# A hybrid encoder step on one core: the sample's attention moved behind the third block's heads

## What is computed

```python
h = x @ w_in                                  # columns q | k | v | u, 512 each
# group A: stick-breaking attention, 8 heads x 64, strictly causal
z = (q @ k.T) * HD ** -0.5
log_1m = where(mask, log_sigmoid(z) - z, 0)
after = reverse_cumsum(log_1m) - log_1m
a_out = where(mask, exp(log_sigmoid(z) + after), 0) @ v
# group B: trailing means of u over 2, 4, 8, 16 frames, minus the token, times pool_w, scaled
mix = concat([a_out, p_out]) @ w_out
x1 = layer_norm(ALPHA * x + mix, ln1_g, ln1_b)
y = layer_norm(ALPHA * x1 + (silu(x1 @ w_gate) * (x1 @ w_up)) @ w_down, ln2_g, ln2_b)
```

## Time and profile before

| what | value |
|---|---|
| median of three runs | 2768.33 us |
| the profiled execution, device time | 2771.78 us |
| its span, first to last instruction | 2770.0 us |
| TensorE busy | 2630.1 us, 95% |
| VectorE busy | 1553.2 us, 56% |
| ScalarE busy | 1113.1 us, 40% |
| GpSimd busy | 1086.6 us, 39% |
| mean granted TensorE clock | 0.985 of full |

### The profile page before, as it was taken

The page is one execution under the profiler, slowest core; times in us unless marked ns, Lnnn a source line. Parts: engine busy times, 40 slices in busy tenths (PEclk is TensorE's granted clock), DMA queues, the critical chain, the costliest instruction groups (busy, mean ns, idle before and its releaser), DMA issues.

```text
span 2770.0 us, 38693 instructions
## 1 busy us (share of the span) xinstructions
PE 2630.1 (95%) x14512; PEld 2241.8 (81%) x14512; DVE 1553.2 (56%) x2122; ACT 1113.1 (40%) x1902; POOL 1086.6 (39%) x949
## 2 busy tenths in 40 slices
PE   8998898998899999999999999999999998999997
PEld 8977798777777887777778877778878896999996
DVE  4466444776342355787663457777776345533335
ACT  3355324665222225555542245555554213322222
POOL 2344225555231235456533155454553213422222
PEclk9999999999999999999999999999999999999999
DMA  6687955775435524344426244243332712323221
GB/s 192 187 242 213 305 171 170 208 216 139 110 99 154 184 77 129 107 119 133 111 88 218 79 114 120 86 133 103 111 101 84 228 62 78 111 86 92 84 84 71
DMA packets 457799, 373.97 MB, mean 135 GB/s; under 512 B 29063, under 2 KB 390911, under 8 KB 457614
## 3 DMA queue, kind: packets, MB, share of 16 engines
q1 hardware_dynamic: 457614, 371.50, 44.8%
HBM read 303.33 MB, written 68.09 MB: 134 GB/s over the span
## 4 chain that ended last, share of the span: by engine, by line
PE 77%; DVE 8%; issue 5%; ACT 4%; DMA 3%; SPq 1%; POOL 1%; DVEq 0%; ACTq 0%; POOLq 0%
PE bank L1217 33%; PE bank L1237 17%; PE bank L1131 8%; PE bank L1071 7%; PE bank L983 4%; PE bank L1029 4%; PE bank L999 3%; DVE left L1633 2%; ACT bank L1329 1%; ACT beta L1328 1%; DVE acc L1749 1%; DMA gw_lo_raw<-in_w_in_dram 1%; DVE aT L1624 1%; DVE stats L1646 1%; DMA mixT_scratch<-o_lo 1%
## 5 line engine op out<-in xcount | busy, mean ns | idle before, releaser
L1217 PE MATMUL bank<-x1T,gw_hi 128*128 128x512 f32 (+1 forms) x3520 | 945.9, 358 | 3.5 <-issue 2.5
L1217 PEld LDWEIGHTS bank<-x1T,gw_hi 128*128 128x128 f32 x3520 | 609.6, 190 | 85.4 <-issue 3.5
L1217 PE MATMUL bank<-x1T,gw_lo 128*128 128x512 f32 (+1 forms) x1760 | 623.2, 354 | 0.0
L2050 POOL TENSOR_TENSOR beta<-beta,left 128x512 f32<-128x512 f32 (+2 forms) x326 | 359.8, 1104 | 478.1 <-DVE left L1633 477.6
L2071 POOL TENSOR_TENSOR gw_lo<-gw_lo_raw,gw_hi 128x1024 fp32r<-128x1024 f32 x88 | 219.2, 2491 | 570.8 <-ACT gw_hi L1376 570.8
L1633 DVE TENSOR_TENSOR_SCAN left<-bank,left,zero_t 128x512 f32<-128x512 f32 (+2 forms) x326 | 363.8, 1116 | 83.1 <-ACT bank L1329 77.8
L1131 PE MATMUL bank<-x1T,gw_hi 128*128 128x256 f32 (+2 forms) x1472 | 363.2, 339 | 14.1 <-POOL gw_lo L2084 11.2
L1217 PEld LDWEIGHTS bank<-x1T,gw_lo 128*128 128x128 f32 x1760 | 333.0, 189 | 48.3
L1319 ACT ACTIVATE aT<-bank 128x512 fp32r<-128x512 f32 (+2 forms) x326 | 173.8, 533 | 492.2 <-PE bank L999 420.4
L1749 DVE TENSOR_TENSOR acc<-bank,acc 128x512 f32<-128x512 f32 x320 | 216.4, 684 | 229.3 <-PE bank L1237 229.2
L1237 PE MATMUL bank<-dw_hi,hT_hi 128*128 128x512 f32 x748 | 306.9, 410 | 36.7 <-DVE acc L1749 21.1
(11 more groups left out here) (165 smaller groups left out, 3859.8 us busy)
## 6 DMA issues: line engine op xcount, KB each, us to landing
gw_lo_raw<-in_w_gate_dram SPq DMA_DIRECT2D x88, 512.0 KB, 4.1
gw_lo_raw<-in_w_up_dram SPq DMA_DIRECT2D x88, 512.0 KB, 4.0
dw_lo_raw<-in_w_down_dram SPq DMA_DIRECT2D x88, 512.0 KB, 4.5
gw_lo_raw<-in_w_in_dram SPq DMA_DIRECT2D x64, 512.0 KB, 4.8
k_st<-kT_scratch SPq DMA_DIRECT2D x160, 128.0 KB, 4.0
v_st<-v_scratch SPq DMA_DIRECT2D x80, 256.0 KB, 4.2
acc<-in_x_prompt_dram SPq DMA_DIRECT2D x32, 512.0 KB, 7.2
q_st<-qT_scratch SPq DMA_DIRECT2D x128, 128.0 KB, 4.0
```

Of the source, the lines that this page charges most:

```text
L1217: m = pe.matmul(gu_bank(g, n)[:, 0:w], gw[L % 4][a][:, k, :], x1T[x][:, k, first:first + w], start=k == 0 and s == 0, stop=k == KD - 1 and ...
L2050: pool.tensor_tensor(x[:, 0:w], x[:, 0:w], left[n % RL][:, 1:w + 1], ALU.mult).then_inc(a_done, 1)
```

## The change

The six items of the sample move from behind block 1's heads to behind block 2's (SAMPLE_BLOCK 1 to 2), and the weight of 8 goes with them. The second mix begins at slot 312 in place of 372, the third attention at slot 396 in place of 456. The second attention still begins at slot 188 and now ends at 312, the third still ends at 637, and the fourth is as it was.

```diff
-SAMPLE_BLOCK = 1
+SAMPLE_BLOCK = 2
...
-    SAMPLE_AT = BASE[2] - 6 - BASE[1]
+    SAMPLE_AT = BASE[SAMPLE_BLOCK + 1] - 6 - BASE[SAMPLE_BLOCK]
...
-        weights = [8 if k == ATTENTION and g == 1 and SAMPLE_AT <= s <= SAMPLE_AT + 6 else 1 for k, g, s in ticks]
+        weights = [8 if k == ATTENTION and g == SAMPLE_BLOCK and SAMPLE_AT <= s <= SAMPLE_AT + 6 else 1 for k, g, s in ticks]
...
-    A_FROM = [72, 188, 456, 721]
-    M_FROM = [128, 372, 637, 956]
+    A_FROM = [72, 188, 396, 721]
+    M_FROM = [128, 312, 637, 956]
```

## The result

The changed kernel takes 2775.74 us at the median of ten runs (2771.48 to 2781.17); the kernel before, in ten runs beside it, 2768.47 (2766.19 to 2773.07). The ratio is 1.0025, with a 95% interval of 1.0015 to 1.0035: slower by 7.3 us. The profiled execution is the slowest of the ten, 2781.17 us with a span of 2779.4, so of the 9.4 us by which its span exceeds the 2770.0 of before some two are its own.

The account below looks back on a forecast made before the run. TensorE, busy for 95% of the span, was taken as the bound; only its waits and lower clock could move. Density 0, LayerNorm -2.5, keys +4.5 and the rest 0 made +2.0 us: median 2770.3, range 2759 to 2783.

Parts of the forecast that it names:

- slower: Case of a slower kernel, by dense steps (0.24) or by the keys and their clock (0.10): chance 0.34.
- the keys and their clock: Slower rival at the sample's key loads: all their clock falls, +9 for +4.5, giving 2775; chance 0.10.
- the one with 0.24: Slower rival: block 2's dense steps beside down products put VectorE behind, 0.28 us a step, +8.6, 2779; chance 0.24.
- The frame: Whole kernel: TensorE's work stays; only its waiting and its time at a lower clock can move.
- Keys, +4.5: Sample's key loads: leads of two slots change four waits by +2.9 us, one more clock fall adds +1.6.
- The rule of the Trainium skill: Sample's key loads: by the page leads would hardly matter, keys' term 0 and sum -2.5; prediction said the trace disagrees.
- Density, 0: Ordinary attention steps, block 1 thinner and block 2 denser: a step loses 0.19 us at either density, so 0.
- the LayerNorm's -2.5: Block 0's second LayerNorm, pairs 0 and 1 of block 1: fewer steps beside it, -2.5 us, ends -6.3 and 0.
- Values, 0: Sample's value loads: six items over seven slots at the same place in the pair, 0, between -3 and +4.
- The second mix at 0: Second mix, 60 slots earlier, over pairs 2 to 5 of block 0: TensorE loses nothing there, cost 0.
- The relief of the projection: Faster rival's step in block 3's projection: 7 steps leave, attention's losses of 8.7 us fall by 6.
- The faster rival: Projection stretch relieved (-6), LayerNorm excess off wholly (-5), keys only +1: sum -10, 2758 us; chance 0.24.

Follow-up runs that it names:

- the position in the pair: Kernel before, sample still behind block 1, its steps 1 to 5 at the second slot of u0 and g0, 12 slots apart: 2775.93 us, 1.0020.
- the twins behind block 1 and block 2: Same sample places within the pairs, behind block 1 against behind block 2: keys at the fourth slot 0.9979 against 0.9955; keys and values apart 0.9934 against 0.9923.
- the kernel before with late keys: Kernel before, sample still behind block 1, its steps 1 to 5 at the fourth slot of u0 and g0: 2762.27 us, 0.9979.

## Why the prediction was right or wrong

The median of 2775.74 lies in the range, and the forecast of 2770.3 was 5.4 us short. The measured ratio passes the bound of 0.2%, though its interval reaches under it, so the case that came is "slower", to which I gave 0.34, and in it the mechanism with 0.10, the keys and their clock, not the one with 0.24. That the median lies in the range is in part luck: two terms of some size were wrong and took opposite signs. Three differences by the ratios give an estimate of the whole: +5.5 for the position in the pair, +8 for the y stores, which the forecast left out, and -6.6 for the place behind block 2, where it had -2.5. The sum is some +7, as measured; each of the three is uncertain by 3 us. Without the stores in the way the changed kernel takes 2768.56, under the forecast.

- **The frame held.** No matmul was added, TensorE stayed the bound, and the span's difference is what it lost.
- **Keys, +4.5, was mis-sized; the stretch lost +10.5.** The leads themselves were nearly right: in the surroundings of block 0 they gave waits of 4.06, 0.53, 3.80 and 1.12 where 3.1, 0.6, 3.9 and 0.6 were worked out. Two things failed. The second wait, 0.6 forecast, was 3.01, since I costed the lead alone and not the y stores that are on their way when the keys are loaded, in block 1 only (0.47 with the stores elsewhere). And I priced one more clock fall of 1.6; there were two more, behind the second and the third wait, and the one behind the first was twice as deep (3.4), and the clock part of the stretch rose from 5.4 to 10.0 us in the two profiled executions. Over ten executions the mean clock hardly differs (0.9846 for 0.9846 to 0.9851), so of the two the missing stores weigh more. The third wait came out at 2.55, shorter than 3.9, and so it did without the stores (2.56); why it is shorter in block 1 stays open.
- **The rule of the Trainium skill** in "DMA: Bandwidth & Descriptors", "Issuing engines are not separate DMA queues", was misread in the prediction. It says of one DMA that its initiation is usually small beside the transfer, and here one issue takes 5.03 / 8 = 0.63 us where a load lands in 4.0, so the trace agrees. It does not follow that leads hardly matter and that the sum is -2.5: eight issues in a row add up, and a landing of 4.0 us is longer than two slots of 1.4 by itself. The ratios of 1.0025 at two slots, 0.9975 at three and 0.9955 at four show that the lead decides.
- **Density, 0, was wrong as a statement and nearly right as a sum.** The step that failed is reading 0.19 us a step from two unlike stretches as one constant. A denser block 2 alone costs 7 us, most of it beside block 0's LayerNorm. In the change that LayerNorm came to stand beside few steps, and the 96 dense steps ahead of it lost 15.7 + 1.0 us, 0.17 each, no more than the 0.19 of before. Block 1 got thinner (its projection stretch and the pair behind it lost 20.2 before and 17.6 after). So the zero was saved by where the dense steps fell, which the prediction had not reasoned. Together with the LayerNorm's -2.5 the forecast was -2.5; the stretches show -3.7, and the twins behind block 1 and block 2 differ by 6.6 and 2.8 us the same way.
- **Values, 0, came to +2.9** in the profile, inside the bounds of -3 and +4. Idle time is the same, 7.4 for 7.5; the rest is clock, 0.88 for 0.92. The same slots show 0.92 with the keys two slots later and 0.90 with one, and the execution profiled of the changed kernel is the slowest of ten with a clock under their mean, so the term of 0 is not refuted.
- **The second mix at 0** held: 658.4:897.1, which holds it, lost 2.7 us with the end of block 1's steps in it.
- **The rivals.** The dense steps have a real price beside a LayerNorm and, at 1.3 slots, elsewhere; at the spacing of the change the trace shows none. The relief of the projection was small, 0.7 us in the stretch itself and 1.9 in the pair behind it, in place of 6; the stretch lasted 165.0 us for 167 forecast. The faster rival also counts the LayerNorm at -5, where the prediction's own excess is 2.7. Of the waits named for the profile (3, 0.6 and 4 us) the first was about right, and the second and third came out at 3.01 and 2.55.

## What to carry to other kernels

When a step with loads of its own is moved along a hand-written order, note at which slot of the new neighbourhood the issuing queue is let go, and count what stands in the queue between that and the load and what large transfers are still on their way: here one slot of 1.4 us decided 14 us, and four stores 8 us. If a wait of TensorE can't be removed, make it shorter all the same, since the clock can double its price (5.9 us less idle time in the key stretch came with 6.1 us less of clock). Look at what else stands where background work is made denser: beside a LayerNorm it cost 7 us. Moving the density about (thin here, dense there) gave nothing back in two tries.

## What was unexpected of the hardware

The clock of TensorE follows its waits, but the length of a single wait does not tell whether it falls. Behind waits for keys of 1.41, 1.60, 1.65 and, before, 2.03 us the clock stayed at its upper level, 2.4 GHz. Behind 2.19, 2.55, 3.01 and 3.62 us it stood at 1.2 GHz for some 3 to 4 us, and for 7 behind the last. That looks like a mark between 2.03 and 2.19, but other traces do not bear it out. The same wait ahead of the feed-forward part, without a fall in the changed kernel and with one in the kernel with keys one slot later:

```profile
622.52 0.71 PE L1217 MATMUL bank<-x1T,gw_hi 128*128 128x512 f32 x2 [2.54 <-issue]
...
622.00:642.00 20.00, 19.48 (x98) 16.18 (x99) 10.42 (x13) 8.68 (x16) 8.61 (x11) 1.00 0.87 247
```

```profile
618.26 0.76 PE L1226 MATMUL bank<-x1T,gw_hi 128*128 128x512 f32 x2 [2.55 <-issue]
...
617.00:637.00 20.00, 18.74 (x86) 15.61 (x87) 10.30 (x14) 9.10 (x18) 6.96 (x8) 0.91 0.86 233
```

A wait for keys of 1.61 us in the kernel before with late keys also had a fall behind it (0.91 over 746:766), and at the changed kernel's values a wait of 1.38 us stands in a stretch of 0.83 (1410:1430). So shorter waits brought a higher mean clock (0.9871 for 0.9846, ten executions of each kernel), but no length of a wait is shown to be safe.

Four stores of 512 KB, issued 5.7 us ahead of a batch of key loads, made the issues of the batch slower (4.75 us for six of them, 3.73 without the stores) and the wait behind it 2.5 us longer, though the batch did not start later behind its weight load.
